# Two long and two short matmuls in turn in the weight products of a two-block transformer kernel

## The chip, the cores and the metric

The kernel runs on one core of a Trainium2 chip. The metric is the device time of one launch in microseconds, as the median of several runs. Before the change it is 3551.57 us (3 runs, 3550.62 to 3554.24).

## What is computed

Two transformer blocks are applied to 256 tokens of width 2048, in float32. Each is a chain of big products with norms, mixers, attention and gated feed-forward layers in between:

```python
def conv_ffn(h, up, conv_w, conv_b, down):
    hid = causal_dwconv(h @ up.astype(h.dtype), conv_w, conv_b)
    gate, val = jnp.split(hid, 2, axis=-1)
    return (jax.nn.gelu(gate) * val) @ down.astype(h.dtype)
...
def swiglu(h, w_gate, w_up, w_down):
    return (jax.nn.silu(h @ w_gate) * (h @ w_up)) @ w_down
...
        p = h @ w_in[l].astype(h.dtype)
...
    x = x + 0.5 * swiglu(rms_norm_2(x, ffn1_norm), ffn1_w_gate, ffn1_w_up, ffn1_w_down)
```

The weights are 2048 or 5632 rows deep and are read from HBM once, some 610 MB in all. The products with these weights are nearly all of the work.

## The kernel before, in words

Everything is held transposed: the 128 partitions are channels, and the 256 tokens are the columns. A product makes one output tile of 128 channels by 256 tokens from k input tiles (16 of them for a depth of 2048, 44 for 5632, 4 or 8 in the branch products). `Product` cuts the k into chunks of up to 8 (`KG`), and each chunk of weights is one DMA of 128 x 1024 floats into one of four slots (`SLOTS`) of `weights_raw`.

Float32 accuracy is had with the cheaper type fp32r by splitting: a weight is a high part (what fp32r holds) and a low part (the rest), and so is the input. For each slot `split_high` (ScalarE, L257) writes `weights_high`, and `split_low` (VectorE, L264) writes `weights_low`. The input's two parts lie side by side as `parts[:, k, 0, :]` and `parts[:, k, 1, :]`, 256 columns each; in the trace they are `moving_halves`, `gated_halves` or `branch_halves`.

`multiply` is TensorE's loop for one output tile. For each k it issues two matmuls:

- the **long** one (L313): the high weights against both input parts, 512 columns, into both halves of an accumulator bank;
- the **short** one (L315): the low weights against the high input part, 256 columns, into the bank's first half.

A **pair** below is one long and one short, the work of one k. There are 9216 of each in a launch. Each matmul comes with a load of its own 128x128 weights into the array, recorded apart on PEld. After the last short of a chunk `slots_free` is raised, on which `split_high` of a later chunk waits. Before a chunk TensorE waits for `low_ready`, and before a tile for `acc_free`. After a tile `take_cross` (ScalarE, L381) and `take_tile` (VectorE, L387) add the two halves of the bank.

All engines run programs written out by hand: `pe_steps` or `multiply_all` runs `multiply` over the tiles, in hardware loops after the first body. In some stages a hook `before(t, k)` is called ahead of each k of a first tile. It waits until input tile k has been made, and in the stages whose norm is taken from tiles (`Normed` with `sum_tile`, L481, 16 calls in each of three stages) it also issues a small float32 matmul on TensorE. In two other stages (`w_in_stage`, and attention) `beside` puts other small matmuls between chunks.

Of the kernel before, what the change touches and what calls it, by code (L numbers as in the profile page):

```python
# [23 lines left out]
SLOTS = 4  # L24
# [275 lines left out]
def multiply(core, pe, prod, acc, i, t, before=None, beside=None):  # L300

    bank = t % 2

    pe.wait_ge(core.acc_free, i * len(prod.tiles) + (prod.tile0 + t + 1))
    nk_all = prod.tiles[t]
    parts = core.h if prod.parts is None else prod.parts
    for u, (_, k0, nk) in prod.of_tile(t):
        pe.wait_ge(core.low_ready, i * prod.per_body + (prod.chunk0 + u + 1))
        for k in range(nk):
            if before is not None:  # L310
                before(t, prod.first[t] + k0 + k)
            x = parts[:, prod.first[t] + k0 + k, :, :]
            core.nc.tensor.matmul(acc[:, bank, :, :], core.high[:, u % SLOTS, k, :], x,  # L313
                                  start=(k0 + k == 0), stop=False)
            last = core.nc.tensor.matmul(acc[:, bank, 0, :], core.low[:, u % SLOTS, k, :], x[:, 0, :],  # L315
                                         start=False, stop=(k0 + k == nk_all - 1))
        last.then_inc(core.slots_free, 1)
        if beside is not None:
            next(beside, None)


def pe_steps(core, pe, prod, acc, lo=0, hi=None, before=None):

    hi = prod.bodies if hi is None else hi
    if lo == 0 and before is not None:
        for t in range(len(prod.tiles)):
            multiply(core, pe, prod, acc, 0, t, before)
            yield 0, t
        lo = 1
    if hi - lo > 1:  # L330
        with pe.Fori(lo, hi) as i:
            for t in range(len(prod.tiles)):
                multiply(core, pe, prod, acc, i, t)
                yield i, t
    elif hi > lo:
        for t in range(len(prod.tiles)):
            multiply(core, pe, prod, acc, lo, t)
            yield lo, t
# [2354 lines left out]
```

## Time and profile before

| | us |
|---|---|
| median of 3 runs | 3551.57 |
| the profiled execution, its own time | 3581.75 |
| its span, first to last instruction | 3579.6 |
| PE (matmul) busy | 3467.2, 97% |
| PEld (weight load) busy | 2989.3, 84% |
| VectorE busy | 2252.1, 63% |
| ScalarE busy | 1736.0, 48% |
| GpSimd busy | 622.0, 17% |

The profile is of one execution. A matmul record begins when TensorE starts on it; its end is modelled and overlaps the next one's begin. So a busy sum says little of the pace, and the pace is read from begin to begin: either from two rows of the timeline, or as a stretch of time divided by the count of one line's records in it. `PEclk` is the share of TensorE's full clock that was granted in a stretch.

### The profile page before, as it was taken

To read this page: it belongs to the slowest core of one execution; us is meant where nothing else is said; L and a number is where in the kernel's file an instruction comes from. 1 tells how busy PE (TensorE), PEld (TensorE's weight loads), DVE (VectorE), ACT (ScalarE), POOL (GpSimd) and SP (SyncE) were. 2 spreads that over 40 slices of the span, in tenths; PEclk is the share of its full clock that TensorE was granted. 3 is DMA by queue.
4 is the path that set the end of the run, shared out by engine and by line. 5 is a ranking of instruction groups with operands and counts; after the bars stand their busy time and mean duration, and the time that the engine had idled before them with its cause. 6 is when DMAs were issued, how large, how long until landed. Compare 5 with 4: busy or idle time off the path is not lost.

```text
span 3579.6 us, 59583 instructions
## 1 busy us (share of the span) xinstructions
PE 3467.2 (97%) x19486; PEld 2989.3 (84%) x19486; DVE 2252.1 (63%) x2905; ACT 1736.0 (48%) x2561; POOL 622.0 (17%) x585
## 2 busy tenths in 40 slices
PE   8999889999999989999999988899989999999999
PEld 7788778888888878888888877788878888888888
DVE  6767667777754475555555677755668655555544
ACT  4444455555544454444444444444446544444443
POOL 1104121111100021111100166621100111111000
PEclk9999999999999999999999999999999999999999
DMA  5423435555556635555565544454435555555555
GB/s 183 147 95 128 155 139 184 184 184 187 186 184 184 188 137 188 187 186 184 181 188 187 203 142 142 141 189 164 159 133 192 183 185 187 187 186 183 185 184 170
DMA packets 174870, 616.01 MB, mean 172 GB/s; under 512 B 20656, under 2 KB 20816, under 8 KB 174416
## 3 DMA queue, kind: packets, MB, share of 16 engines
q1 hardware_dynamic: 174368, 609.84, 50.3%
q10 hardware_dynamic: 432, 5.24, 0.4%
q8 instruction: 43, 0.70, 0.1%
q14 instruction: 27, 0.22, 0.0%
HBM read 610.81 MB, written 4.19 MB: 172 GB/s over the span
## 4 chain that ended last, share of the span: by engine, by line
PE 86%; DVE 6%; POOL 4%; issue 2%; ACT 1%; DMA 0%; DVEq 0%; ACTq 0%; SPq 0%; POOLq 0%
PE acc L313 54%; PE acc L315 27%; POOL x_T L2349 2%; POOL x_T L2352 1%; DVE x_T L2304 1%; DVE weights_low L264 1%; ACT weights_high L257 1%; POOL x_T L2350 0%; DVE x_T L2309 0%; DVE x_T L2306 0%; DVE x_T L2302 0%; PE ps_narrow L2083 0%; PE ps_wide L2059 0%; DVE arena L606 0%; DVE halves_memory L606 0%
## 5 line engine op out<-in xcount | busy, mean ns | idle before, releaser
L313 PE MATMUL acc<-moving_halves,weights_high 128*128 128x512 f32 x6848 | 2467.9, 405 | 20.7 <-DVE moving_halves L522 15.6
L264 DVE TENSOR_TENSOR weights_low<-weights_raw,weights_high 128x1024 fp32r<-128x1024 f32 (+1 forms) x1184 | 1461.3, 1242 | 822.6 <-ACT weights_high L257 820.6
L315 PE MATMUL acc<-moving_halves,weights_low 128*128 128x256 f32 x6848 | 1930.0, 282 | 0.0
L257 ACT ACTIVATE weights_high<-weights_raw 128x1024 fp32r<-128x1024 f32 (+1 forms) x1184 | 1220.6, 1033 | 857.8 <-PE acc L315 843.0
L313 PEld LDWEIGHTS acc<-moving_halves,weights_high 128*128 128x128 f32 x6848 | 1297.8, 190 | 353.5 <-issue 26.0
L315 PEld LDWEIGHTS acc<-moving_halves,weights_low 128*128 128x128 f32 x6848 | 1305.5, 191 | 9.1 <-issue 7.6
L313 PE MATMUL acc<-gated_halves,weights_high 128*128 128x512 f32 x2112 | 746.4, 399 | 0.0
L315 PE MATMUL acc<-gated_halves,weights_low 128*128 128x256 f32 x2112 | 593.5, 281 | 0.0
L381 ACT ACTIVATE cross_products<-acc 128x256 f32<-128x256 f32 x512 | 195.3, 381 | 715.7 <-PE acc L315 715.7
L313 PEld LDWEIGHTS acc<-gated_halves,weights_high 128*128 128x128 f32 x2112 | 397.2, 188 | 98.7
L404 POOL TENSOR_TENSOR stage_scratch<-unscaled,token_scale 128x256 f32<-128x256 f32 x264 | 216.8, 821 | 1272.0 <-DVE unscaled L387 807.0
L315 PEld LDWEIGHTS acc<-gated_halves,weights_low 128*128 128x128 f32 x2112 | 399.8, 189 | 0.0
L387 DVE TENSOR_TENSOR unscaled<-acc,cross_products 128x256 f32<-128x256 f32 x400 | 169.2, 423 | 360.1 <-ACT cross_products L381 360.0
L404 POOL TENSOR_TENSOR arena<-unscaled,token_scale 128x256 f32 (+1 forms) x116 | 112.7, 971 | 524.4 <-DVE unscaled L387 488.6
L441 POOL TENSOR_TENSOR squares_total<-squares_total,squares 128x256 f32<-128x256 f32 x60 | 46.5, 775 | 557.0 <-ACT squares L428 557.0
L2349 POOL TENSOR_TENSOR x_T<-x_T,trig 32x512 f32<-32x512 f32 x20 | 95.5, 4775 | 65.3 <-DVE x_T L2314 65.3
L313 PE MATMUL acc<-branch_halves,weights_high 128*128 128x512 f32 x256 | 90.5, 399 | 0.0
L865 DVE SCALAR_TENSOR_TENSOR arena<-stage_scratch,vectors,arena 128x256 f32<-128x256 f32 x88 | 63.7, 723 | 22.8 <-ACT arena L832 21.3
L943 ACT ACTIVATE gated_halves<-stage_scratch 128x256 f32 (+1 forms) x88 | 36.8, 418 | 84.0 <-DVE stage_scratch L964 84.0
L315 PE MATMUL acc<-branch_halves,weights_low 128*128 128x256 f32 x256 | 71.9, 281 | 0.0
L2374 PE MATMUL ps_scale<-x_T,constants 128*128 128x512 f32 x40 | 24.1, 688 | 36.2 <-ACT x_T L2233 36.2
L313 PEld LDWEIGHTS acc<-branch_halves,weights_high 128*128 128x128 f32 x256 | 48.1, 188 | 11.9
(321 smaller groups left out, 1570.8 us busy)
## 6 DMA issues: line engine op xcount, KB each, us to landing
weights_raw<-in_w_in SPq DMA_DIRECT2D x272, 512.0 KB, 3.4
weights_raw<-in_ffn_up SPq DMA_DIRECT2D x176, 512.0 KB, 3.7
weights_raw<-in_ffn_w_gate SPq DMA_DIRECT2D x176, 512.0 KB, 3.5
weights_raw<-in_ffn_w_up SPq DMA_DIRECT2D x176, 512.0 KB, 4.4
weights_raw<-in_ffn_w_down SPq DMA_DIRECT2D x160, 512.0 KB, 3.7
weights_raw<-in_ffn_down SPq DMA_DIRECT2D x80, 512.0 KB, 4.1
weights_raw<-in_w_out SPq DMA_DIRECT2D x64, 512.0 KB, 3.5
weights_raw<-in_ffn_w_down SPq DMA_DIRECT2D x32, 256.0 KB, 2.6
```

Of the source, the lines that this page charges most:

```text
L257: core.nc.scalar.activation(core.high[:, slot, 0:nk, :].rearrange("p a b -> p (a b)"), core.raw[:, slot, 0:nk * P], ACT.Copy).then_inc(cor ...
L264: core.nc.vector.tensor_tensor(core.low[:, slot, 0:nk, :].rearrange("p a b -> p (a b)"), core.raw[:, slot, 0:nk * P], core.high[:, slot, 0 ...
L313: core.nc.tensor.matmul(acc[:, bank, :, :], core.high[:, u % SLOTS, k, :], x, start=(k0 + k == 0), stop=False)
L315: last = core.nc.tensor.matmul(acc[:, bank, 0, :], core.low[:, u % SLOTS, k, :], x[:, 0, :], start=False, stop=(k0 + k == nk_all - 1))
L381: core.nc.scalar.activation(core.cross[:, t % 2, :], acc[:, t % 2, 1, :], ACT.Copy).then_inc(core.cross_ready, 1)
L387: core.nc.vector.tensor_tensor(out, acc[:, t % 2, 0, :], core.cross[:, t % 2, :], ALU.add).then_inc(core.acc_free, 1)
L404: core.nc.gpsimd.tensor_tensor(out, core.z[:, t % 2, :], core.rs[:, :], ALU.mult).then_inc(core.z_free, 1)
L441: core.nc.gpsimd.tensor_tensor(core.total[:, :], core.total[:, :], core.sq[:, t % 2, :], ALU.add).then_inc(core.squares_used, 1)
L865: nc.vector.scalar_tensor_tensor(conv[:, t, :], hidden[:, t, PAD - 1:PAD - 1 + S], tap(i, t, 1), conv[:, t, :], ALU.mult, ALU.add).then_in ...
L943: nc.scalar.activation(g_parts[:, i, 0, :], g, ACT.Copy).then_inc(core.g_high, 1)
L2304: nc.vector.scalar_tensor_tensor(tmp, tmp, -0.5, var, ALU.mult, ALU.mult).then_inc(own, 1)
L2349: nc.gpsimd.tensor_tensor(swap, swap, each(trig[:, 1, :]), ALU.mult).then_inc(pool_own, 1)
```

## The change

In each chunk the k are taken in twos. Both long matmuls are issued first, for k and k+1, then both short ones. The sums, the shapes, the data, the waits and their counts stay as they are, and so does everything on the other engines.

```diff
-        for k in range(nk):
-            if before is not None:
-                before(t, prod.first[t] + k0 + k)
-            x = parts[:, prod.first[t] + k0 + k, :, :]
-            core.nc.tensor.matmul(acc[:, bank, :, :], core.high[:, u % SLOTS, k, :], x,
-                                  start=(k0 + k == 0), stop=False)
-            last = core.nc.tensor.matmul(acc[:, bank, 0, :], core.low[:, u % SLOTS, k, :], x[:, 0, :],
-                                         start=False, stop=(k0 + k == nk_all - 1))
+        for pair in range(0, nk, 2):
+            ks = range(pair, min(pair + 2, nk))
+            for k in ks:
+                if before is not None:
+                    before(t, prod.first[t] + k0 + k)
+                core.nc.tensor.matmul(acc[:, bank, :, :], core.high[:, u % SLOTS, k, :],
+                                      parts[:, prod.first[t] + k0 + k, :, :], start=(k0 + k == 0), stop=False)
+            for k in ks:
+                last = core.nc.tensor.matmul(acc[:, bank, 0, :], core.low[:, u % SLOTS, k, :],
+                                             parts[:, prod.first[t] + k0 + k, 0, :],
+                                             start=False, stop=(k0 + k == nk_all - 1))
```

How it moves TensorE's instructions, first inside a plain chunk. Before, from the first matmul of a chunk on (its wait is in brackets):

```order
L313 MATMUL acc<-moving_halves_49,weights_high 128x512 [waits low_ready]
L315 MATMUL acc<-moving_halves_49,weights_low 128x256
L313 MATMUL acc<-moving_halves_49,weights_high 128x512
L315 MATMUL acc<-moving_halves_49,weights_low 128x256
L313 MATMUL acc<-moving_halves_49,weights_high 128x512
```

And with the change (its lines are numbered three and fewer further on; "x2" is two alike in a row):

```order
L314 MATMUL acc<-moving_halves_49,weights_high 128x512 [waits low_ready]
L314 MATMUL acc<-moving_halves_49,weights_high 128x512
L317 MATMUL acc<-moving_halves_49,weights_low 128x256 x2
L314 MATMUL acc<-moving_halves_49,weights_high 128x512 x2
L317 MATMUL acc<-moving_halves_49,weights_low 128x256 x2
```

Long and short no longer alternate. The wait for the chunk stays on its first matmul, and the last of a chunk is still a short one.

Second, in a first tile with the hook, where `sum_tile` stands between the pairs. Before, from the start of the program:

```order
L481 MATMUL ps_scale<-squares,constants 128x256 [waits low_ready,squared,acc_free,inputs_loaded]
L313 MATMUL acc<-moving_halves_49,weights_high 128x512 [waits part_low]
L315 MATMUL acc<-moving_halves_49,weights_low 128x256
L481 MATMUL ps_scale<-squares,constants 128x256 [waits squared]
L313 MATMUL acc<-moving_halves_49,weights_high 128x512 [waits part_low]
L315 MATMUL acc<-moving_halves_49,weights_low 128x256
```

And with the change:

```order
L484 MATMUL ps_scale<-squares,constants 128x256 [waits low_ready,squared,acc_free,inputs_loaded]
L314 MATMUL acc<-moving_halves_49,weights_high 128x512 [waits part_low]
L484 MATMUL ps_scale<-squares,constants 128x256 [waits squared]
L314 MATMUL acc<-moving_halves_49,weights_high 128x512 [waits part_low]
L317 MATMUL acc<-moving_halves_49,weights_low 128x256 x2
```

The short matmul of an even k now stands behind the waits for input tile k+1 and behind that tile's small matmul.

## Rows read from the trace of the kernel before

**Rows 1.** The page: busy time, then the chain that ended last, by engine and line.

```profile
PE 3467.2 (97%) x19486; PEld 2989.3 (84%) x19486; DVE 2252.1 (63%) x2905; ACT 1736.0 (48%) x2561; POOL 622.0 (17%) x585
...
PE 86%; DVE 6%; POOL 4%; issue 2%; ACT 1%; DMA 0%; DVEq 0%; ACTq 0%; SPq 0%; POOLq 0%
PE acc L313 54%; PE acc L315 27%; POOL x_T L2349 2%; POOL x_T L2352 1%; DVE x_T L2304 1%; DVE weights_low L264 1%; ACT weights_high L257 1%; POOL x_T L2350 0%; DVE x_T L2309 0%; DVE x_T L2306 0%; DVE x_T L2302 0%; PE ps_narrow L2083 0%; PE ps_wide L2059 0%; DVE arena L606 0%; DVE halves_memory L606 0%
```

**Rows 2.** Stretches, L313 alone: from:to, length, busy (count), clock, DMA share, GB/s.

```profile
512.00:1250.00 738.00, 738.00 (x2090) 392.89 (x2089) 1.00 0.56 185
...
1281.00:2026.00 745.00, 745.00 (x2110) 396.60 (x2109) 1.00 0.55 186
...
2736.00:2835.50 99.50, 99.30 (x282) 52.79 (x281) 1.00 0.55 190
2835.50:3575.00 739.50, 739.50 (x2095) 393.60 (x2094) 1.00 0.55 184
330.00:364.70 34.70, 34.70 (x101) 18.80 (x101) 1.00 0.45 159
...
2666.20:2670.00 3.80, 3.74 (x6) 1.94 (x7) 0.50 0.02 4
```

**Rows 3.** Timeline of PE in a long stretch: start us, us, operation.

```profile
1500.21 0.40 PE L313 MATMUL acc<-moving_halves,weights_high 128*128 128x512 f32 x1
1500.45 0.28 PE L315 MATMUL acc<-moving_halves,weights_low 128*128 128x256 f32 x1
1500.57 0.40 PE L313 MATMUL acc<-moving_halves,weights_high 128*128 128x512 f32 x1
1500.81 0.28 PE L315 MATMUL acc<-moving_halves,weights_low 128*128 128x256 f32 x1
1500.92 0.40 PE L313 MATMUL acc<-moving_halves,weights_high 128*128 128x512 f32 x1
1501.15 0.28 PE L315 MATMUL acc<-moving_halves,weights_low 128*128 128x256 f32 x1
1501.27 0.40 PE L313 MATMUL acc<-moving_halves,weights_high 128*128 128x512 f32 x1
```

**Rows 4.** Timeline of PE, the stretch from 330.00 on.

```profile
330.07 0.39 PE L313 MATMUL acc<-moving_halves,weights_high 128*128 128x512 f32 x1
330.31 0.28 PE L315 MATMUL acc<-moving_halves,weights_low 128*128 128x256 f32 x1
330.42 0.40 PE L313 MATMUL acc<-moving_halves,weights_high 128*128 128x512 f32 x1
330.65 0.28 PE L315 MATMUL acc<-moving_halves,weights_low 128*128 128x256 f32 x1
330.77 0.39 PE L313 MATMUL acc<-moving_halves,weights_high 128*128 128x512 f32 x1
```

**Rows 5.** Timeline of PE after a long wait, at half the clock.

```profile
2666.18 0.63 PE L313 MATMUL acc<-moving_halves,weights_high 128*128 128x512 f32 x1
...
2666.82 0.63 PE L313 MATMUL acc<-moving_halves,weights_high 128*128 128x512 f32 x1
```

**Rows 6.** Timeline of the weight loads, PEld, beside rows 3.

```profile
1500.45 0.19 PEld L313 LDWEIGHTS acc<-moving_halves,weights_high 128*128 128x128 f32 x1
1500.57 0.19 PEld L315 LDWEIGHTS acc<-moving_halves,weights_low 128*128 128x128 f32 x1
```

**Rows 7.** Timeline of PE: matmuls of 16 and 8 columns, each with its own weights.

```profile
52.76 0.26 PE L1252 MATMUL ps_narrow<-ba_halves,moving_halves 128*128 128x16 f32 x1
52.87 0.25 PE L1254 MATMUL ps_narrow<-ba_halves,moving_halves 128*128 128x8 f32 x1
52.98 0.26 PE L1252 MATMUL ps_narrow<-ba_halves,moving_halves 128*128 128x16 f32 x1
```

**Rows 8.** Waits: engine line, waited for: us in total, times, longest us.

```profile
ACT weights_high L257 <- PE acc L315: 843.0, 583, 11.7
DVE weights_low L264 <- ACT weights_high L257: 820.6, 703, 9.3
```

**Rows 9.** Timeline of PE in a first tile with `sum_tile`.

```profile
1271.55 0.51 PE L313 MATMUL acc<-moving_halves,weights_high 128*128 128x512 f32 x1 [0.22 <-DVE moving_halves L524]
1271.89 0.28 PE L315 MATMUL acc<-moving_halves,weights_low 128*128 128x256 f32 x1
1272.01 0.59 PE L481 MATMUL ps_scale<-squares,constants 128*128 128x256 f32 x2
1272.82 0.50 PE L313 MATMUL acc<-moving_halves,weights_high 128*128 128x512 f32 x1 [0.22 <-DVE moving_halves L524]
```

## The prediction

> **What bounds the kernel now.** I began with the page. TensorE's matmuls are busy for 97% of the span, and the chain that ended last is 86% TensorE, 54% of it the long matmuls and 27% the short ones [rows 1]. No other engine has more than 6% of that chain. The list of waits says the same from the other side: the split of the high weights sat waiting for TensorE's last short matmul of a chunk for 843 us, and the split of the low weights for that split for 821 us [rows 8]. Weights are ready before TensorE wants them, so nothing that feeds it needs to be counted, and an edit in its own order counts in full.
>
> Next I wanted TensorE's pace. Four long stretches have nothing but products in them: 738.0, 745.0, 99.5 and 739.5 us with 2090, 2110, 282 and 2095 long matmuls [rows 2]. A count takes in one record that overlaps an edge, so these are about 6573 pairs in 2322 us, 353.3 ns each. Three pairs on the timeline say it again: 1500.21 to 1501.27 is 1.06 us [rows 3]. All 9216 pairs at this pace would be 3256 us, 91% of the span. **One nanosecond on a pair is 9.2 us of the kernel.**
>
> Then I asked what a pair ought to take. At a granted clock of 0.50, 1.2 GHz [rows 2], a pair takes 0.64 us [rows 5], which is its 768 columns at one column per cycle and nothing more. At the full 2.4 GHz the same 768 columns would be 320 ns, so of the 353.3 ns some 33 are lost to something other than columns. That loss is what the order of the matmuls may touch.
>
> The pace is not even a constant. In the stretch from 330.0 to 364.7 us the same instructions at the same full clock make about 100 pairs in 34.7 us, 347 ns each [rows 2], and the timeline there has two pairs in 0.70 us, rounded to hundredths [rows 4]. Begin to begin, a long takes 0.23 or 0.24 us and a short 0.11 or 0.12 us in both places, and which values follow each other makes the difference [rows 3, 4]. Each stretch keeps its pace to its end, 738 us in one case. So the alternation of long and short settles into a rhythm, one of at least two, and all four long stretches sit in the slower one. DMA traffic does not decide it: the fast stretch has 159 GB/s and the slow ones about 185, but a pace that never drifts within a stretch is not what a varying traffic would make.
>
> **The change, part by part.** It adds no instruction and removes none; the listing of the new order shows the same matmuls regrouped.
>
> *Weight loads.* Each load begins with the matmul ahead of it: loads at 1500.45 and 1500.57, matmuls at the same two times [rows 6, 3]. So one load, never two, hides beside one matmul. Matmuls of 16 and 8 columns, which are nothing but their loads, follow each other in 0.11 us [rows 7]. That is the price of a load at the full clock, and it is just about the time of a short matmul: 256 columns are 107 ns at 2.4 GHz, and a short takes 0.11 to 0.12. Before, per pair, one load lies beside a long and one beside a short. After, over two pairs, two loads lie beside longs and two beside shorts. The same loads have the same covers. If the cost is simply a sum over matmuls, the change is worth 0.
>
> *The rhythm.* What does change is who follows whom: long after long, short after short, as well as both old steps. No row shows the two new steps at this rate. I bound each by the rows nearest to it. A long takes 0.23 to 0.24 us whatever followed it, and a short 0.11 to 0.12, so a pair lies between 0.34 and 0.36 us. With the pairs outside the long stretches (9216 - 6573 = 2643, in fast and slow rhythms mixed, which I put at 350 ns) the bounds are: at 340 ns, 6573 x -13.3 + 2643 x -10 = -114 us; at 360 ns, 6573 x 6.7 + 2643 x 10 = +70 us. Between the ends I take 350 ns, the middle of the two and also the middle of the two rhythms seen (347 and 353.3): with the alternation gone the new pattern has no reason to land in the slow rhythm each time. That is 6573 x -3.3 = -22 us.
>
> *Slots.* The last matmul of a chunk is still a short one with the same signal, so the splits are released when they were. Four slots and 843 us of waiting [rows 8] cover any shift of 0.1 us. 0.
>
> *First tiles with the hook.* The short of an even k now waits for input tile k+1 and its small matmul. A round there lasts 1.27 us (1271.55 to 1272.82), of which the long and the short are 0.46 [rows 9], and TensorE then waits for VectorE's next input tile. Shifting 0.12 us of short within a round whose length VectorE sets costs nothing until the end of the tile, where one more short is left over: 0.12 us in each of some eight such tiles, +1 us.
>
> *The sum.* -22 + 1 = -21 us against the profiled execution, whose own time is 3581.75 us. The median of the runs is 3551.57, that is 30 us or 0.8% lower. I can't see where these 30 us lie. If they were all pace they would be 3.3 ns on a pair, and then the unprofiled runs would already be near 349 ns, with little left to win. I therefore take half of the gain, -10 us: **3541 us**.
>
> On weight loads the Trainium skill (TensorE: Matmul & The Clock Gate, section "LDWEIGHTS (loading the stationary operand)") gives columns / 1.2 in nanoseconds, 107 ns for these 128. By that, the load would be hidden behind a short only just, and its sum is the same 0; the trace's 0.11 us per load agrees.
>
> **The rivals.** 0.2% (7 us, 0.8 ns on a pair) is about what a measurement of this kernel can tell from no change.
>
> *A. The pace is a plain sum.* Each matmul costs its own time whatever stands beside it, and the order is worth nothing but the +1 us. For it: same loads, same covers, same columns. Against it: the same instructions show two paces [rows 2]. It gives 3552 to 3553 us. The Trainium skill (the same page, section "Back-to-back issue gap") has such a rule, N/2.4 + 2.5 ns for a matmul alone, 325 ns for a pair, in which order plays no part; the trace does not agree with its size, 353.3 against an estimate of 325.
>
> *B. The fast rhythm throughout.* Two longs in a row leave a load ample time, and everything settles at 347 ns: 6573 x -6.7 + 2643 x -3.3 = -53 us, 3499 us. For it: this pace exists at full clock. Against it: nothing says that the new order prefers it, and the runs without a profile may have it in part already.
>
> *C. Two shorts in a row are worse than one (the slower side).* The load of the second short can start only when the first short starts, and that of the next long only with the second short. A load is as long as a short [rows 7, 3]; so any lateness of a load, from sharing its reads with the columns of the matmul beside it, adds up over two shorts, where before a long came after each to take it up. Price: a short at 0.12 in place of the mean of 0.116, and a long after it at 0.24, gives pairs of up to 0.36 us. It decides from the point where a pair passes 354 ns. At a middle of 356.7 ns it is 6573 x 3.3 + 2643 x 6.7 = +39 us, 3591 us; at its end, +70, 3622 us. For it: two of three shorts in the slow rhythm already show 0.12 [rows 3]. Against: in the fast stretch they don't all.
>
> That the change is not what it says is ruled out by the listing of the new order.
>
> **How the numbers follow.** My forecast, a mixed pace near 350 ns, has 0.35; A has 0.15, B 0.20, C 0.30. Faster by over 0.2%: all of B and 0.22 of the forecast, 0.42. Slower: C and 0.03 of the forecast, 0.33. The same: A and 0.10 of the forecast, 0.25. The range: B's 3499 with a little beyond for 340-ns pairs in part, and C's 3591 with a little beyond, 3490 to 3600. Outside are B's extreme (3438) and C's (3622), together 0.2. The chances are spread over both signs, so the forecast's own range is narrower: 3520 to 3556.
>
> **What the profile would show.** In the same long stretches, time over the count of long matmuls gives the pace at once: 350 for the forecast, 353.3 for A, 347 for B, over 354 for C. On the timeline, long to long and short to short stand alone for the first time; if long to long is 0.22 or less, or short to short is over 0.12, my bounds were wrong. The waits of the splits for TensorE should stay near 840 us. The prediction is wrong if the pace moves out of 340 to 360 ns, or if TensorE starts to wait for `low_ready`.

## The result, and the profile after

The kernel with the change takes 3547.09 us (median of 20 runs, 3544.70 to 3551.08). The kernel before took 3567.26 us in 20 runs, the three of before the change among them. One of them took 4219.88 us; it is left out of the ratio and of every count below. The other 19 are spread from 3538.55 to 3588.24, with a median of 3566.59. The ratio is 0.9945, with a 95% interval of 0.9929 to 0.9960: faster by 0.55%, about 20 us. The forecast was faster, 3541 us, with a range from 3490 to 3600.

Three things are to be seen at once: a gain, a spread of 6 us in place of some 50, and a best run of before (3538.55) that is faster than any run after.

The page of the changed kernel, busy time and chain, beside [rows 1]:

```profile
span 3543.7 us, 59583 instructions
...
PE 3430.6 (97%) x19486; PEld 2972.0 (84%) x19486; DVE 2247.9 (63%) x2905; ACT 1736.5 (49%) x2561; POOL 623.2 (18%) x585
...
PE 85%; DVE 6%; POOL 4%; issue 2%; ACT 1%; DMA 0%; DVEq 0%; ACTq 0%; SPq 0%; POOLq 0%
```

Nothing has taken TensorE's place. Its profiled execution took 3545.77 us, 36.0 less than the 3581.75 of before.

The same long stretches as in [rows 2], and two short ones that were fast before (columns: from:to, length, busy and count of the long matmul L314, busy and count of its loads, clock, DMA share, GB/s):

```profile
510.00:1238.00 728.00, 656.34 (x2091) 318.14 (x2090) 1.00 0.58 188
1269.00:2003.00 734.00, 661.81 (x2108) 320.78 (x2108) 1.00 0.58 188
2713.00:2808.00 95.00, 85.63 (x273) 41.64 (x274) 1.00 0.58 191
2810.50:3539.00 728.50, 656.82 (x2092) 318.24 (x2092) 1.00 0.58 187
104.50:134.00 29.50, 26.62 (x86) 12.87 (x85) 1.00 0.52 177
329.50:364.50 35.00, 31.55 (x102) 15.22 (x100) 1.00 0.50 161
```

With one count taken off for the record that overlaps an edge, as in the prediction, 728.00 / 2090 is 348.3 ns a pair, 734.00 / 2107 is 348.4, and 728.50 / 2091 is 348.4. The 35.0-us stretch has 346.5 by this sum, where one count more or less is 3.5 ns; from the begins of its own matmuls it is 348.3. **All six stretches now have one pace, 348.3 ns.** The four long ones had 353.3 before: 6573 x -5.0 = -33 us of the 36.

The timeline of PE there (two alike in a row are one row, "x2", so starts are one per two matmuls), beside [rows 3]:

```profile
1500.29 0.63 PE L314 MATMUL acc<-moving_halves,weights_high 128*128 128x512 f32 x2
1500.76 0.40 PE L317 MATMUL acc<-moving_halves,weights_low 128*128 128x256 f32 x2
1500.99 0.63 PE L314 MATMUL acc<-moving_halves,weights_high 128*128 128x512 f32 x2
1501.46 0.39 PE L317 MATMUL acc<-moving_halves,weights_low 128*128 128x256 f32 x2
1501.68 0.62 PE L314 MATMUL acc<-moving_halves,weights_high 128*128 128x512 f32 x2
```

Two longs take 0.47 us and two shorts 0.23 or 0.22; from 1500.29 to 1501.68 there are four pairs in 1.39 us. The trace keeps begins in whole nanoseconds, finer than the timeline prints them, and numbers to the nanosecond below are means of these. The cycle repeats every four pairs: begin to begin, the four longs are 233, 236, 232 and 231 ns, the four shorts 116, 113, 113 and 119.

The splits still wait for TensorE, 817 and 803 us where [rows 8] has 843 and 821. They wait 26 and 17 us less, while TensorE got 36 us faster:

```profile
ACT weights_high L257 <- PE acc L317: 817.0, 547, 11.5
DVE weights_low L264 <- ACT weights_high L257: 803.3, 698, 9.3
```

### The profile page after: what moved, and what is told of

Same layout as the page of the kernel before. It is cut to its first block, busy times and chain, and to the rows that moved or that the text cites. A ratio compares the mean times of both kernels' runs of the same rounds, so it can differ in the third digit from the quotient of the medians.

```text
span 3543.7 us, 59583 instructions
## 1 busy us (share of the span) xinstructions
PE 3430.6 (97%) x19486; PEld 2972.0 (84%) x19486; DVE 2247.9 (63%) x2905; ACT 1736.5 (49%) x2561; POOL 623.2 (18%) x585
## 4 chain that ended last, share of the span: by engine, by line
PE 85%; DVE 6%; POOL 4%; issue 2%; ACT 1%; DMA 0%; DVEq 0%; ACTq 0%; SPq 0%; POOLq 0%
PE acc L314 54%; PE acc L317 27%; POOL x_T L2352 2%; POOL x_T L2355 1%; DVE weights_low L264 1%; DVE x_T L2307 1%; ACT weights_high L257 1%; POOL x_T L2353 0%; DVE x_T L2312 0%; DVE x_T L2309 0%; DVE x_T L2305 0%; PE ps_narrow L2086 0%; PE ps_wide L2062 0%; DVE arena L609 0%; DVE halves_memory L609 0%
## 5 line engine op out<-in xcount | busy, mean ns | idle before, releaser
L314 PE MATMUL acc<-moving_halves,weights_high 128*128 128x512 f32 x6848 | 2201.4, 402 | 20.8 <-DVE moving_halves L525 15.6
L317 PE MATMUL acc<-moving_halves,weights_low 128*128 128x256 f32 x6848 | 1353.6, 279 | 0.0
L314 PEld LDWEIGHTS acc<-moving_halves,weights_high 128*128 128x128 f32 x6848 | 1058.0, 190 | 50.7 <-issue 33.1
L314 PE MATMUL acc<-gated_halves,weights_high 128*128 128x512 f32 x2112 | 663.3, 395 | 0.0
L317 PE MATMUL acc<-gated_halves,weights_low 128*128 128x256 f32 x2112 | 414.9, 278 | 0.0
L390 DVE TENSOR_TENSOR unscaled<-acc,cross_products 128x256 f32<-128x256 f32 x400 | 169.3, 423 | 347.6 <-ACT cross_products L384 347.5
L314 PEld LDWEIGHTS acc<-gated_halves,weights_high 128*128 128x128 f32 x2112 | 321.5, 189 | 0.0
L314 PE MATMUL acc<-branch_halves,weights_high 128*128 128x512 f32 x256 | 80.4, 395 | 0.0
L317 PEld LDWEIGHTS acc<-branch_halves,weights_low 128*128 128x128 f32 x256 | 48.1, 188 | 11.4
L484 PE MATMUL ps_scale<-squares,constants 128*128 128x256 f32 x96 | 33.6, 436 | 24.3 <-DVE squares L599 14.7
```

Of the source, the lines that this page charges most:

```text
L390: core.nc.vector.tensor_tensor(out, acc[:, t % 2, 0, :], core.cross[:, t % 2, :], ALU.add).then_inc(core.acc_free, 1)
```

## The experiments

The question was why the order of equal work changes the pace. Theory R (rhythm): a matmul's length depends on where in a fine grid of time it begins; a repeated order settles into a cycle on that grid, and some orders have more than one. Theory T (turns): each turn from long to short and back costs something, and fewer turns help. Theory S is rival C of the prediction: shorts in a row run late. All kernels differ in `multiply` alone. Each diff is against the changed kernel or, where it takes the alternation as its start (the mirror order, half of the weights per load, and two of the orders in the last group), against the kernel before.

### The kernel before, once more

No edit; a second profile of it.

> The kernel before once more, for a second profile. Theory R: each of the long stretches (three of about 2100 pairs) takes the slow or the fast rhythm by chance of where it starts, 14 us apart each, so this execution's time tells beforehand how many are fast: near 3582 none, near 3567 one, near 3553 two, near 3538 all three. If instead all stretches show 353.3 and the time is near 3553, the spread of before has another cause.

It took 3538.84 us. Stretches of L313:

```profile
512.00:1237.00 725.00, 725.00 (x2092) 391.02 (x2091) 1.00 0.58 189
1267.00:1998.00 731.00, 731.00 (x2109) 394.26 (x2110) 1.00 0.58 189
2709.00:2805.00 96.00, 96.00 (x278) 51.91 (x278) 1.00 0.59 192
2807.00:3532.00 725.00, 725.00 (x2092) 391.03 (x2092) 1.00 0.58 188
2643.00:2658.00 15.00, 15.00 (x43) 7.91 (x43) 1.00 0.38 123
```

725.00 / 2091 is 346.7 ns, and 731.00 / 2108 is 346.8: all four long stretches, slow in [rows 2], are fast here, in the same program. Only a small one, from 2643 us, is slow (15.0 us with 42 to 43 pairs; from the begins of its matmuls, 353 ns). It is one run, with the profile on. The clock is 1.00 in both rhythms, and DMA traffic is higher here, 189 GB/s, than the 185 of the slow stretches in [rows 2]. So neither the clock nor more traffic makes the slow rhythm. The timeline has four pairs in 1.39 us, where [rows 3] has three in 1.06:

```profile
1499.89 0.39 PE L313 MATMUL acc<-moving_halves,weights_high 128*128 128x512 f32 x1
1500.12 0.28 PE L315 MATMUL acc<-moving_halves,weights_low 128*128 128x256 f32 x1
1500.24 0.39 PE L313 MATMUL acc<-moving_halves,weights_high 128*128 128x512 f32 x1
...
1501.28 0.39 PE L313 MATMUL acc<-moving_halves,weights_high 128*128 128x512 f32 x1
```

The two rhythms are cycles of different length. Begin to begin, long and short in turn, every pair of this run's long stretches takes 230 and 117 ns; the slow stretches of [rows 2] repeat every three pairs, 241 and 120, 236 and 113, 233 and 117, which is 1060 ns.

The times of all runs of before agree with this. The three big stretches have about 2100 pairs each, and 2100 x 6.67 ns is 14 us, so the time should fall on steps of 14 us. The 99 runs of before that were taken beside the change and beside the experiments do:

| runs | from, to (us) | middle (us) | big stretches in the slow rhythm |
|---|---|---|---|
| 4 | 3538.55, 3540.55 | 3539.3 | none |
| 38 | 3549.42, 3557.82 | 3553.3 | one |
| 41 | 3561.95, 3571.50 | 3568.3 | two |
| 16 | 3578.65, 3588.24 | 3582.4 | three |

The last column is shown by a profile for the first and the last band (3538.84 and 3581.75 us). For the middle two it is inferred from the steps. What picks the rhythm of a stretch no run shows. (The expectation had named the bands by their fast stretches; the count is the same.)

### The mirror order

```diff
+        for k in range(nk):
+            if before is not None:
+                before(t, prod.first[t] + k0 + k)
+            for long in ((True, False), (False, True))[k % 2]:
...
```

Each round of the inner loop issues the long or the short matmul of k as before; the last one issued in a chunk, now a long, signals `slots_free`.

> Long, short, short, long in each two k, so that the sequence over many k is again two long, two short, but each chunk and tile now ends and begins with a long, and the waits stand in the middle of two longs. Theory R and theory T: the cyclic order alone decides, so the pace is 348.3 ns a pair as with the change, and the time is within 5 us of the change's 3547. If instead the place of the chunk's wait sets the pace, it will be another one, 346.7 or 353.3.

3546.79 us (10 runs, 3544.79 to 3549.61), ratio to before 0.9955 (0.9930 to 0.9980). Its stretch 509.50 to 1238.00 is 728.5 us with 2092 longs, 348.4 ns, and it repeats the change's cycle to the nanosecond, though every chunk's wait now stands between two longs. So the cyclic order sets the pace, not the place of the waits or of the first tile's hooks.

### Larger groups: threes, fours, eights

```diff
-        for pair in range(0, nk, 2):
-            ks = range(pair, min(pair + 2, nk))
+        for pair in range(0, nk, 4):
+            ks = range(pair, min(pair + 4, nk))
```

and the same with 8. The threes take the eight k of a chunk as 3, 3 and 2.

> The k are taken in fours: four long matmuls, then four short ones. Theory R (rhythm): each order of long and short settles into one cycle of its own on a fixed grid of about 6.7 ns, whatever the share of alternations; the pace is then some value between 343 and 353 ns a pair, the same in all long stretches, and it need not be below the 348.3 of the change. Theory T (turns): what costs is each turn from long to short and back, 5 ns a pair for two turns before and half of that with the change in twos; halving the turns again gives about 346 ns and some 20 us less than the change. Theory S (shorts in a row are late): pace above 350 ns, and the third and fourth short at 120 ns or more.

> A whole chunk at a time: eight long matmuls, then eight short ones. Theory R: again one constant pace in all long stretches, between 343 and 353 ns a pair, not ordered by group size. Theory T: below that of the fours, about 344.5 ns a pair, some 35 us under the change. Theory S: above the fours.

> Per chunk of eight: groups of three, three and two. Between twos (348.3) and fours (350.8) if the pace went smoothly with the size of the group, about 349.5 ns a pair; theory R makes no order among them and allows 347 to 352, but one pace in all stretches.

| groups of | median of 10 runs (us) | range | ratio to before (95%) | pace in the first long stretch (ns) |
|---|---|---|---|---|
| 2 (the change, 20 runs) | 3547.09 | 3544.70 to 3551.08 | 0.9945 (0.9929, 0.9960) | 348.3 |
| 3 | 3556.58 | 3554.99 to 3559.95 | 0.9985 (0.9959, 1.0011) | 349.6 |
| 4 | 3565.01 | 3564.42 to 3572.51 | 1.0008 (0.9982, 1.0034) | 350.7 |
| 8 | 3557.80 | 3554.39 to 3559.99 | 0.9975 (0.9951, 0.9999) | 349.1 |

The base of a ratio is before's mix of rhythms in that sitting (its medians lie between 3557.82 and 3567.26), so the orders are better compared by their own times and paces; the change and the mirror order, from two sittings, agree within 0.3 us. Three of the ten runs of the fours lie at 3569.7 to 3572.5, the other seven at 3564.4 to 3566.8; whether a second rhythm is behind that no profile shows.

Theory T is refuted: halving the turns from twos to fours makes the kernel 18 us slower. Theory S is right in one half. The fours are above 350 ns, but the eights are below the fours, not above them. In the timeline of the eights, eight shorts take 0.96 us (1500.14 to 1501.10), 120 ns each, as it said; but eight longs take 1.84 us (1501.10 to 1502.94), 230 each, and make up for it:

```profile
1500.14 1.12 PE L317 MATMUL acc<-moving_halves,weights_low 128*128 128x256 f32 x8
1501.10 2.00 PE L314 MATMUL acc<-moving_halves,weights_high 128*128 128x512 f32 x8
1502.94 1.11 PE L317 MATMUL acc<-moving_halves,weights_low 128*128 128x256 f32 x8
```

### All matmuls long

```diff
-                last = core.nc.tensor.matmul(acc[:, bank, 0, :], core.low[:, u % SLOTS, k, :],
-                                             parts[:, prod.first[t] + k0 + k, 0, :],
+                last = core.nc.tensor.matmul(acc[:, bank, :, :], core.low[:, u % SLOTS, k, :],
+                                             parts[:, prod.first[t] + k0 + k, :, :],
```

> The low weights are multiplied with both parts of the input too, so that every matmul has 512 columns; this adds the product of the two low parts. Two matmuls are 426.7 ns of columns at the full clock. If each long costs about 233 ns whatever follows (20 ns over its columns, one load beside each), the two take 466 ns. If the loss belongs to the turns between unequal matmuls, the two take 216 ns each, about 432 ns. If the loss is made up beside the second half of a long, it lies between.

4440.38 us. Its first stretch (here L314 is half of the matmuls):

```profile
597.00:1545.00 948.00, 644.00 (x2092) 392.67 (x2092) 1.00 0.46 144
```

948.00 / 2091 is 453.4 ns for two, between the 432 and the 466 of the expectation: 226.7 each, 13.3 ns over the 213.3 of the columns. Eight shorts in a row were 13.3 over their 106.7. So a matmul among its like costs its columns and 13.3 ns, and a pair made of these is 346.7, just the fast rhythm. In the slow rhythm and at the turns of the grouped orders something is added: of the eights, the first five longs after a turn take 233, 236, 228, 233 and 231 ns and the last three 227, while the first short after the turn takes 113 and the last six 120.

### Half of the weights per load

```diff
+            m = P if k0 + k in (0, nk_all - 1) else P // 2
+            core.nc.tensor.matmul(acc[0:m, bank, :, :], core.high[:, u % SLOTS, k, 0:m],
...
+            last = core.nc.tensor.matmul(acc[0:m, bank, 0, :], core.low[:, u % SLOTS, k, 0:m],
```

> The order of before, but in all k of a tile other than its first and its last only 64 of the 128 stationary columns are loaded and used (half of the output channels miss those k); the columns streamed stay 512 and 256. If the loss of 13.3 ns per matmul is taken by the load's own reads, half a load costs half: a pair of 320 + 2 x 6.7 = 333 ns, with or without one grid step of 6.7 on top. If the loss is a fixed price of a switch of weights, the pair stays at 346.7 or 353.3.

> Both matmuls of a k with 512 columns, where the full width took 226.7 ns each, and now 64 stationary columns in all k of a tile but its first and last. Loss by the load's reads: 220 ns each. Loss by a fixed price per switch: 226.7 ns each.

Both kernels leave out half of the output channels in all k of a tile but its first and last, and each was run once. In the order of before (3486.92 us) the first stretch:

```profile
506.50:1218.00 711.50, 711.50 (x2090) 288.92 (x2089) 1.00 0.59 192
```

711.50 / 2089 is 340.6 ns a pair. Away from the whole loads at a tile's ends every pair takes 340.0, the long 227.5 and the short 112.5, where the fast rhythm has 230 and 116.7. With all matmuls long (4496.45 us):

```profile
598.00:1560.00 962.00, 823.25 (x2091) 291.80 (x2091) 1.00 0.45 142
```

962.00 / 2090 is 460.3 for two, 230 each, which is more than with whole loads. The alternation gains 6 to 13 ns from halved loads, and its 340.0 is what the expectation gave to the loads' reads with one grid step on top (333 + 6.7). But the longs lose 3.5 ns each where the same theory had them gain 6.7, so neither theory of the expectations explains both runs. The two runs with long matmuls alone also differ in their order (two high, two low with whole loads; high and low in turn with halves), and no run separates that from the load. What the 13.3 ns are made of stays open.

### Breaking the alternation now and then

The order of before for six k of a chunk, and the last two as a group:

```diff
+        for k in range(nk - 2):
...
+        for k in (nk - 2, nk - 1):
```

> The order of before (long, short in turn) for all k of a chunk but the last two, and only these two grouped as in the change. Theory R, with rhythms that lock: the grouped two shift the phase once a chunk; if a shift returns the alternation to the same rhythm every time, every long stretch has one and the same pace and the runs lie within 3 us of each other, as with the change. The pace is 346.7 ns a pair if the fast rhythm is the one that it returns to, 353.3 if the slow one. Theory T (turns cost, so fewer turns help): a quarter of the change's gain, about 352 ns in every stretch.

3558.89 us (10 runs, 3555.16 to 3560.31), ratio 0.9979 (0.9962 to 0.9995). All long stretches have one pace, 349.7 ns, and it is none of those expected (346.7, 353.3, or 352 by the turns): the trace has one chunk fast and the next slow, in turn. In its timeline (L312 is a long of the six alone, here the first of a chunk, L319 a grouped one) the six take 2.08 us in one chunk, 600.66 to 602.74, and 2.12 in the next, 603.44 to 605.56, that is 347 and 353 ns each:

```profile
600.66 0.40 PE L312 MATMUL acc<-moving_halves,weights_high 128*128 128x512 f32 x1
...
602.74 0.63 PE L319 MATMUL acc<-moving_halves,weights_high 128*128 128x512 f32 x2
...
603.44 0.40 PE L312 MATMUL acc<-moving_halves,weights_high 128*128 128x512 f32 x1
...
605.56 0.63 PE L319 MATMUL acc<-moving_halves,weights_high 128*128 128x512 f32 x2
```

A group of two flips the rhythm that it meets. That the alternation can be steered at all is what theory R says; that a group would always lead into the same rhythm was wrong. Three more orders tried to use it. The first two (and the threes above) take the chunk's k in groups of these sizes:

```diff
+        k1 = 0
+        for size in ((1, 1, 1, 1, 2, 2) if nk == KG else (1, 1, 2)):
+            ks = range(k1, k1 + size)
+            k1 += size
...
```

with (1, 1, 2, 1, 1, 2) in the second and (3, 3, 2) in the threes. The third turns one k of each chunk:

```diff
+            for long in ((False, True) if k == nk - 1 else (True, False)):
```

> Per chunk of eight: four k in the order of before, then two groups of two. With one group per chunk the trace showed that a group turns the fast rhythm into the slow one and the slow into the fast. Theory R, by which the rhythm after a group follows from the phase in which it begins: two groups in a row turn it twice, so an alternation that is fast stays fast, and as four k are not a whole number of the slow cycle (three k), a slow one may be thrown into it. Then all stretches have 4 pairs at 346.7 and 4 at 348.3, 347.5 ns a pair, and the time is some 3540 us, 7 under the change. If a slow alternation stays slow, stretches differ again: 347.5 or 350.8 ns. If rhythms don't matter and only the number of turns does: between before and the change in every stretch, near 351 ns.

> Per chunk of eight: two k in the order of before and a group of two, twice. Theory R: another single cycle, somewhere between 346.7 and 353.3 ns a pair; a group that follows only two alternating k never meets a whole slow cycle, so I expect it near the change, 348 to 350 ns, the same in all stretches. If only the number of turns counts: about 350.8 ns.

> The order of before, with only the last k of each chunk turned round (short, then long), so that two shorts and then two longs stand together once a chunk, in the reverse sense of the group in twos. Theory R: the turned k shifts the rhythm once a chunk. With the group in twos it flipped fast into slow and back (349.7 ns a pair everywhere, 3559 us). If this one flips too, again about 350 ns and one pace; if it keeps what it finds, two paces and runs spread over 40 us as before; if it always leads into the fast rhythm, about 347 ns in all stretches, runs within 5 us of each other near 3540 us, which would beat the change. If only the number of turns counted, it would be like the single group in twos, 349.7.

- Four k alone and two groups of two: 3565.10 us (3557.01 to 3578.04), ratio 1.0023 (0.9998 to 1.0048). Two rhythms in one execution:

```profile
2736.00:2832.00 96.00, 91.32 (x277) 46.92 (x277) 1.00 0.59 192
2834.50:3570.00 735.50, 697.71 (x2088) 355.90 (x2088) 1.00 0.57 185
```

  96.00 / 276 is 347.8 ns, the 347.5 expected where the alternation is fast, and 735.50 / 2087 is 352.4 where it is slow, more than the 350.8 expected: there the first group's two pairs take 713 ns, not 697. Two flips keep what they find, and four k alone don't throw it into the fast one.
- Two k alone and a group of two, twice: 3572.27 us (3569.69 to 3575.98), ratio 1.0026 (1.0003 to 1.0049). 735.0 us with 2091 longs in the first stretch is 351.7 ns, and 736.5 with 2106 in the second is 349.9: two rhythms again, where one near 348 to 350 was expected.
- The last k turned: 3577.46 us (12 runs, 3575.82 to 3580.25), ratio 1.0038 (1.0019 to 1.0056), one pace of 352.3 ns. It is the slowest of all orders by its median, with a spread of only 4 us, and one pace was expected at 347 or 350.

No order that was run beats the change in the median; the mirror order equals it. The alternation has the better best case, 3539 us, in 4 runs of 99.

What these runs show of theory R is that orders settle into repeating cycles, that some have more than one, and that a group can switch between them. That a matmul's length follows from where it begins on a fine grid fits all paces but was not tested apart from them.

## Why the prediction was right, point by point

**TensorE's own pace counts in full.** Right. Of 36.0 us between the two profiled executions 33 are the pace in the four long stretches. The waits of the splits shrank as TensorE got faster, and nothing else became the bound.

**Two rhythms, and the slow one in all four stretches.** Right, and it carried the forecast. What I did not draw from it is that the rhythm is chosen anew in each stretch and in each run. The second profile shows it for the stretches, and the steps of 14 us for the runs. The reason given against DMA traffic was only argued; the second profile settles it, with the fast rhythm at 189 GB/s.

**The new steps between 0.34 and 0.36 us a pair, 350 ns taken.** The bounds held, and the value was too high: the measured pace is 348.3 ns in every stretch, -33 us in place of -22. Nor is it a mix: the forecast was "a mixed pace", and all stretches are alike. No reason for 350 was more than the middle of two ends; it can't be worked out from the rows before. The signs that would have shown the bounds wrong did not come: a long before a long takes 232 to 233 ns, a short before a short 113 to 116.

**The 30 us between the profiled execution and the median.** The prediction said "I can't see where these 30 us lie", and took half of the gain. They were rhythm. The profiled execution had all three big stretches slow, the band near 3582, and the first three runs, near 3552, were in the band of one slow stretch. Over 99 runs the number of slow stretches is 168 of 297, so before has on average 346.7 + 0.57 x 6.7 = 350.5 ns in them, and the change gains 2.2 x 6573 = 14 us there. The measured 20 us have 6 more. Part of these are the pairs in the other stretches, and the median of before's runs beside the change lies 3 to 4 us over the mean of the 99, 3563.5; I did not split them further. The forecast's -10 us was this term mis-sized: taking a half was a guess, and a list of runs with steps in it would have told better. The sentence beside it has a slip too: 3.3 ns less than 353.3 is 350, not 349.

**How close the number came.** That 3541 lies 6 us from 3547 is in part luck. The base of 3551.57 was 12 us under the mean of before's runs, the draw of three runs in the band of one slow stretch, and the gain of 10 was some 6 us too small against that mean. The two errors pull opposite ways.

**Weight loads.** Their count beside longs and shorts is unchanged, as said. The rule of the Trainium skill for a matmul alone (TensorE: Matmul & The Clock Gate, section "Back-to-back issue gap"), N/2.4 + 2.5 ns, makes an estimated 325 ns a pair, whatever the order. The runs disagree in both: 346.7 to 353.3 ns for the same work, by order and by chance.

**First tiles with the hook, +1 us.** Too small to be seen in the times. In a first tile the rounds stay near 1.27 us (a long at 1257.66, the next at 1258.93), with the two shorts after it:

```profile
1257.66 0.50 PE L314 MATMUL acc<-moving_halves,weights_high 128*128 128x512 f32 x1
1258.00 0.59 PE L484 MATMUL ps_scale<-squares,constants 128*128 128x256 f32 x2
1258.93 0.50 PE L314 MATMUL acc<-moving_halves,weights_high 128*128 128x512 f32 x1 [0.34 <-DVE moving_halves L527]
1259.26 0.40 PE L317 MATMUL acc<-moving_halves,weights_low 128*128 128x256 f32 x2
```

**The rivals.** A, a plain sum, is refuted by the second profile of before, 43 us faster than the first with no edit, and by the orders of the experiments, 348.3 to 352.3 ns a pair for the same matmuls. B, 347 ns throughout, is what before does in 4 runs of 99; the change stays 1.7 ns over it. C has its late shorts, 120 ns in groups of eight, but in the change's groups of two they take 113 to 119, and the pace is under before's slow one, not over it.

## What to carry to other kernels

When the same instructions show two paces at the same clock, look at the run times of many executions before anything else: steps in them that equal pairs times the difference of pace mean that a single profile shows one draw, and the base of a comparison is their mix. An order in which only one rhythm is seen can beat, in the median, one whose best is better, and it makes every later comparison sharper (a spread of 6 us in place of 50). The pace of an order is to be measured and not reasoned from its neighbours: twos, threes, fours and eights gave 348.3, 349.6, 350.7 and 349.1 ns in no order.

## What the runs showed of the hardware that was not expected

- Alternating fp32r matmuls of 512 and 256 columns, each with a load of 128 columns, run at 346.7 or 353.3 ns a pair at the full clock and keep to it for 2100 pairs, though each chunk of eight is supplied on its own.
- The paces seen are multiples of one step of 6.67 ns (353.33 - 346.67) over whole cycles: 52 and 53 steps a pair for the alternation, 209 for four pairs of the change, 68 for two longs, 18 for a short among shorts. What the step belongs to is not shown.
- A matmul among its like costs its columns and 13.3 ns, for 512 columns and for 256. With half of the load's columns the alternation is faster (340.6 ns) and the row of longs slower (230 each in place of 226.7, in another order of high and low). Why is open.
